# Two transformer-like blocks on one core: six places for raw weight chunks and five split buffers, in place of eight and four

## The reference

```
h = rmsnorm(x, g) * (1 + scale) + shift          # tokens; hc likewise for 256 context tokens
q, k, v, up, uf, g = split_proj(h @ w_in)        # 1024 | 256 | 256 | 512 | 512 | 2048 columns
att  = attention(rope(norm(q)), [kc ; k], [vc ; v])   # 8 heads, 2 key heads, blocks of 128 queries
pool = windowed means minus token, mapped        # 4 groups of 128
four = real 2-D DFT of groups of 128, mapped
x   += gate * ((concat(att, pool, four) * silu(g)) @ w_out)
```

## Time and profile before

| | |
|---|---|
| median of 3 runs | 2350.74 us |
| the profiled execution | 2353.96 us |
| its span, first to last instruction | 2352.1 us |
| mean granted TensorE clock | 0.986 |
| busy: PE, DVE, ACT, POOL | 97%, 55%, 44%, 11% |
| DMA read | 428.89 MB, 185 GB/s over the span |

### The profile page before, as it was taken

How to read it: one execution, slowest core, us unless ns; L and a number is a source line. 1 busy time by engine, 2 the same in 40 slices (tenths; PEclk the granted TensorE clock), 3 DMA queues, 4 the chain that set the end, 5 groups by cost and what they waited for, 6 DMA issues and landing times.

```text
span 2352.1 us, 30034 instructions
## 1 busy us (share of the span) xinstructions
PE 2271.9 (97%) x11859; PEld 1832.5 (78%) x11859; DVE 1297.0 (55%) x2046; ACT 1040.3 (44%) x1592; POOL 266.7 (11%) x326
## 2 busy tenths in 40 slices
PE   5989999999999989999999998999999999999998
PEld 2567777777777867678888887888888888888887
DVE  3333453442432364555777776677755777567764
ACT  2222333432321255445554565555544555345553
POOL 1001100000010122100020324111100111001111
PEclk8999999999999999999999998999999999999999
DMA  9874443345655475735566544565656565666653
GB/s 357 316 277 167 147 144 110 110 142 172 224 178 179 148 273 192 238 96 159 182 208 203 176 139 152 179 197 180 188 191 194 182 186 187 197 188 187 188 190 116
DMA packets 322428, 437.14 MB, mean 186 GB/s; under 512 B 13849, under 2 KB 220113, under 8 KB 321265
## 3 DMA queue, kind: packets, MB, share of 16 engines
q1 hardware_dynamic: 316800, 413.19, 54.2%
q0 software_dynamic: 3392, 16.90, 2.0%
q10 hardware_dynamic: 2096, 5.15, 0.6%
HBM read 428.89 MB, written 6.29 MB: 185 GB/s over the span
## 4 chain that ended last, share of the span: by engine, by line
PE 85%; DVE 5%; ACT 4%; DMA 3%; issue 2%; POOL 1%; SPq 0%; ACTq 0%; POOLq 0%
PE ps L1361 24%; PE ps L1362 12%; PE ps L1336 8%; PE ps L1338 8%; PE ps L1337 8%; PE ps L1356 5%; PE ps L1358 5%; PE ps L1357 5%; PE ps L1316 3%; ACT SPL L1567 2%; DVE SPL L1818 2%; DMA RAW<-in_w_in_dram 2%; PE ps L1410 1%; PE ps L1427 1%; DMA RAW<-in_ada_w_dram 1%
## 5 line engine op out<-in xcount | busy, mean ns | idle before, releaser
L1818 DVE TENSOR_TENSOR SPL<-RAW,SPL 128x1024 fp32r<-128x1024 f32 x592 | 752.6, 1276 | 637.9 <-ACT SPL L1567 635.3
L1361 PE MATMUL ps<-HS,SPL 128*128 128x512 f32 x2688 | 959.8, 401 | 10.4 <-DVE SPL L1818 7.5
L1567 ACT ACTIVATE SPL<-RAW 128x1024 fp32r<-128x1024 f32 x592 | 621.7, 1055 | 451.2 <-PE ps L1338 174.0
L1362 PE MATMUL ps<-HS,SPL 128*128 128x256 f32 x2688 | 756.6, 281 | 0.0
L1361 PEld LDWEIGHTS ps<-HS,SPL 128*128 128x128 f32 x2688 | 507.9, 189 | 136.1 <-DVE SPL L1818 5.3
L1362 PEld LDWEIGHTS ps<-HS,SPL 128*128 128x128 f32 x2688 | 511.0, 190 | 2.0 <-issue 1.7
L1336 PE MATMUL ps<-SPL,HS 128*128 128x512 f32 x960 | 396.6, 413 | 18.7 <-DVE HS L1867 6.6
L1338 PE MATMUL ps<-SPL,HS 128*128 128x512 f32 x960 | 379.2, 395 | 0.0
L1337 PE MATMUL ps<-SPL,HS 128*128 128x512 f32 x960 | 378.7, 394 | 0.0
L1336 PEld LDWEIGHTS ps<-SPL,HS 128*128 128x128 f32 x960 | 183.2, 191 | 83.0 <-issue 28.6
L1337 PEld LDWEIGHTS ps<-SPL,HS 128*128 128x128 f32 x960 | 183.4, 191 | 41.3 <-issue 5.3
(11 more groups left out here) (289 smaller groups left out, 1691.2 us busy)
## 6 DMA issues: line engine op xcount, KB each, us to landing
RAW<-in_w_in_dram SPq DMA_DIRECT2D x208, 512.0 KB, 5.7
RAW<-in_ada_w_dram SPq DMA_DIRECT2D x192, 512.0 KB, 5.0
RAW<-in_ffn_w_up_dram SPq DMA_DIRECT2D x192, 512.0 KB, 3.6
RAW<-in_w_out_dram SPq DMA_DIRECT2D x96, 512.0 KB, 4.7
RAW<-in_ffn_w_down_dram SPq DMA_DIRECT2D x96, 512.0 KB, 4.2
x_spill<-XT POOLq DMA_DIRECT2D x2, 2048.0 KB, 15.0
XT<-x_spill POOLq DMA_DIRECT2D x1, 4096.0 KB, 16.6
MM<-in_x_dram ACTq DMA_DIRECT2D x2, 1024.0 KB, 10.8
```

The source lines that it names most:

```text
L1361: mm(PS[b][:, :], wr, hh, start=k == 0, stop=False, skip_group_check=True)
L1362: m = mm(PS[b][:, 256:512], wl, hh[:, 0:256], start=False, stop=k == KT - 1, skip_group_check=True)
L1567: act(SPL[:, (n - 1) % NSPL, 0, :], raw_of(i), ACT.Copy).then_inc(s_hi, 1)
L1818: tt(w[:, 1, :], raw_of(s["i"]), w[:, 0, :].bitcast(F32), ALU.subtract).then_inc(s_lo, 1)
```

## The change

Three constants change, and nothing else. Raw places go from eight to six, split buffers from four to five (two raw places are as large as one split buffer, which has two halves), and the window of the splits outside the opening from five positions to six.

```diff
-NRAW = 8
-NSPL = 4
-AHEAD = 5
+NRAW = 6
+NSPL = 5
+AHEAD = 6
 START_AHEAD = 3
 FILL = 6
 OPENING = 74
```

## The result

The changed kernel takes 2537.61 us (median of 6 runs, 2531.8 to 2549.0), the kernel before, timed beside it, 2351.47 us (6 runs, 2347.99 to 2352.85). The ratio is 1.0796, 95% interval 1.0776 to 1.0816: 186 us slower, where +169 was forecast.

A forecast was written before the change was run, and what follows sets the result against it. The prediction took the kernel to be bound by PE's own work, busy 2271.9 of 2352.1 us. Its terms, 72 + 36 + 5 + 8 + 56 - 8, gave +169, so 2520 us, range 2362 to 2610.

The forecast's parts named there:

- The mechanism: Stretches with ada chunks: ACT and DVE stand at splits whose loads were just issued, side tasks queue behind; 72% chance.
- The period's steps: One attention period: first load lands 4.0 us after issue, ACT free at 7.5, DVE at 8.8; 4.2 us lost.
- Layer 0: Projections after the opening: side tasks held in attention, head norms, pool and Fourier cost 72 us in 19 periods.
- Layer 1 and the joint: Layer 1 loses 3 us in twelve periods, 36; the joint between the layers loses 5 us.
- The clock: Slower TensorE clock after stalls: 18 of 31 stalled periods at 3.1 us each, 56 us; bounds 0 and 105.
- The opening: Start of the kernel: less load cushion makes a projection chunk's split some 1 us late in eight groups, 8 us.
- The output product: Layer 0's 14 pairs in the output product: no side task there feeds PE, so 0 us.
- The fifth buffer: Stretches without ada chunks: splits planned four chunks ahead, not three, removing PE's split waits; gain 8 us, bounds 0 and 16.
- only the edges: Rival, 11%: stalls in the ada stretches are covered, only joint and opening lose; 2355 to 2385 us.
- faster: Rival, 5%: the extra split removes PE's split waits and loads still come in time; 2339 us.
- no change: Rival, 3%: the extra lead is never used and the two places never missed; within 0.2%, 2351 us.
- dearer: Rival, 9%: layer 1's periods grow by 5 us each and every stall brings the slow clock; +285, 2635 us.

The follow-up runs named there:

- 6/5/4: Kernel before with six raw places instead of eight, five split buffers instead of four, window four instead of five: 2360.2 us, ratio 1.0045.
- the two kernels with seven places: Kernel before with seven raw places instead of eight, four split buffers: 2453.0 us with window six, 2362.8 us with window five.
- 8/4/6: Kernel before with only the window changed, five to six; eight raw places and four split buffers kept: 2359.6 us, ratio 1.0036.
- 6/5/5: Kernel before with six raw places instead of eight and five split buffers instead of four, window still five: 2470.9 us, ratio 1.0509.
- 6/4/5: Kernel before with only raw places changed, eight to six; four split buffers and window five kept: 2464.8 us, ratio 1.0487.

## Why the prediction was right, and where not

- *The mechanism* was right and is shown: the bursts begin with w_in, ACT and DVE stand at the head of the pair, and side tasks wait behind them. 6/5/4 and the two kernels with seven places show that it is the split's place in ACT's list against the release of its load.
- *The period's steps.* First landing 3.6 us after issue (4.0 forecast), ACT free at A + 7.1 (7.5), DVE at A + 8.4 (8.8), L1410 at A + 11.0 (A + 11.0). L1427 was said to wait for ACT's copy to A + 8.2; it waited for DVE to empty the bank, to A + 8.7. The wrong releaser with nearly the right time, since both stand behind the same splits.
- *Layer 0*: 72 us idle forecast, 71.8 measured. Cut at the starts of the runs of ada chunks, PE's idle time grew by 1 us or more in 21 periods from 136 to 532 us (19 forecast). By what PE waits for in them:

| what PE waits for | periods and idle us forecast | measured |
|---|---|---|
| attention, L1427 (with some L1410 behind it) | 7, 29 | 7, 28.2 |
| attention, L1410 alone | 3, 8 | 2, 4.0 |
| head norms, L1402 | 4, 19 | 5, 21.5 |
| pool and Fourier, L1438 to L1465 | 5, 16 | 5, 14.4 |
| a split, and tiles of h, L1336 | none | 2, 3.7 |

So the terms hold one by one, and not the total alone. That it agrees to 0.2 us is luck: single periods of one kind lie apart (2.96 to 5.05 us at L1427, where 4.2 was forecast for each), and what was too low makes up for what was too high.
- *Layer 1 and the joint*: 41 forecast, 36.4 measured. In layer 1 ten periods grew, by 2.5 to 5.4 us, 35.7 in all, and one shrank by 1.5 (twelve at 3, 36, forecast). The working divided 143 us by 16 pairs, with the joint in it; the periods themselves are 8.25 us on average. At the joint the first product came 4.4 us later (4.2 forecast), but the ada result behind it, 9.53 us after the run of ada chunks began, now came 12.77 after it: 3.2 lost, not 5, since the 3.41 us wait there went into the new one.
- *The clock*: 56 us forecast, 59.5 measured as PE's extra busy time. The stalled periods are 31, as many as forecast; 4.4 of the 59.5 us stand in the opening and aren't shown to be the clock. The granted clock of the layer 0 stage fell from 0.99 to 0.91, below the 0.95 forecast, and that of layer 1 from 0.98 to 0.88. Each is a mix of 1.2 and 2.4 GHz. That the size came out is in part luck: the extra busy time of a stalled period in layer 0 goes from nothing to 3.35 us, where 3.1 in 18 of them was taken.
- *The opening*: 8 us forecast before the clock, 5.8 idle measured, 10.2 with PE's busy time.
- *The output product*, costed at 0, lost 6.2. "No side task that feeds PE" was wrong: one wait of 6.5 us, of L1356 for a tile by DVE L1999, stands there, ahead of the output product's first chunk (behind the pair at 617.6 us before, 740.0 after), behind splits that wait for w_out (101.1 us on ACT, 20.7 before). The stage from 966 to 1247 lost 6.0, forecast at nothing. By PE's landmarks 4.9 of them are lost from 966 to 980 us of the kernel before, right behind the last pair of ada chunks: PE waits three times there, 4.5 us in all, where it waited 1.58 us before.
- *The fifth buffer* is the step that failed in kind: "-8" and "PE's waits at L1361 are gone". They fell from 7.5 to 6.2 us. The wait of 4.74 us in the recurrence is the same in both kernels; first before, then after:

```profile
1422.28 0.76 PE L1361 MATMUL ps<-HS,SPL 128*128 128x512 f32 x1 [4.74 <-DVE SPL L1818]
```

```profile
1611.08 0.80 PE L1361 MATMUL ps<-HS,SPL 128*128 128x512 f32 x1 [4.81 <-DVE SPL L1818]
```

In the changed kernel the window of six spends the fifth buffer on planning a chunk earlier, and each split still waits for the chunk just multiplied. DVE reaches that low half with the same backlog. My own sentence had said that ACT and DVE do the same work at the same times; the "one chunk more in reserve" that I drew from it isn't there when DVE is behind. With a window of four the split of chunk p + 3 waits for chunk p - 2, done a chunk earlier, and then the buffer brings its 12.6 us, though not at L1361 either, where PE still waits 8.0 us. So no run shows the gain in the place where the term of -8 saw it. The recurrence and what follows were 4.5 us shorter in the changed kernel, but not by idle time, which grew by 1.7.

The balance, in idle time: forecast 72 + 36 + 5 + 8 - 8 = 113, measured 125.0. Too low were the fifth buffer (-8, and +1.7 from 1247 us on), the output product (0 and 4.8) and 966 to 1247 (0 and 4.5), by 19.0; too high the joint with layer 1, the opening and layer 0, by 7.0. The clock adds 3.5. So 169 became 184.5 in the profiled executions, and 186 by the medians. The rivals are out: "only the edges" ended at 2385, "faster" and "no change" at 2351, and "dearer" wanted 80 us of idle time in layer 1 and 105 us of slow clock, where some 36 and 59.5 came.

The Trainium skill, "DMA: Bandwidth & Descriptors" (Rules for kernel authors), says to issue a DMA early and to wait on its semaphore late. The runs here agree with it, and either half is nearly enough: with the load as late as in the changed kernel and the wait two positions later, 177 of the 186 us are back (6/5/4, 2360.2 us); with the wait as early as in the changed kernel and the load early, 178 are (8/4/6, 2359.6 us; it has four split buffers). Only the two together cost.

## What to carry to other kernels

When a ring gets shorter or a window longer, don't count the spare places: work out, for each kind of chunk, which chunk's completion releases its load (the latest one among all loads ahead in that queue), and what of PE's work lies between that and the place at which an in-order engine stands for it. If it takes PE less time than a landing (3.6 us here for the first load of a burst), every task behind that place waits too. A buffer added together with a longer window may be spent by the window; try it with the window shortened: with the window held it gave nothing here (6/5/5 against 6/4/5).

## What I had not expected of the hardware

- Short waits came with nearly half as much again in slower matmuls: 125.0 us of added idle time with 59.5 us more of PE's busy time. The stretch of 10 us after the joint, which had 0.81 before, shows it; the windows of after:

```profile
946.00:956.00 10.00, 5.27 (x31) 2.85 (x24) 3.07 (x4) 2.47 (x4) 0.93 (x2) 0.79 0.84 297
956.00:966.00 10.00, 7.77 (x27) 5.59 (x29) 5.96 (x12) 8.01 (x15) 3.69 (x6) 0.70 0.34 125
```

- A load of 512 KB at a DMA queue that had nothing under way lands 3.6 to 3.8 us after its issue (425.24 to 428.85, 946.73 to 950.55), the next 1.4 to 1.5 us behind it. The two kinds differ by their place in the burst: w_in, now in front, has a median of 4.2 us and ada 6.4, where the kernel before, with ada in front, had 4.6 for ada and 6.7 for w_in (median from 360 to 460 us):

```profile
RAW<-in_w_in_dram SPq DMA_DIRECT2D x10, 512.0 KB, 4.2
RAW<-in_ada_w_dram SPq DMA_DIRECT2D x10, 512.0 KB, 6.4
```
